# The cross-attention keys computed with stationary tokens and turned by DVE and ACT

## The reference

```python
memn = rms_norm(mem, norm_mem_g[l])
# cross_attend(rms_norm(x, norm2_g[l]), memn, wq, wk, wv, wo):
q = (xn @ wq).reshape(B, S, XA_HEADS, XA_HEAD_DIM)
k = (memn @ wk).reshape(B, M, XA_HEADS, XA_HEAD_DIM)
v = (memn @ wv).reshape(B, M, XA_HEADS, XA_HEAD_DIM)
scores = jnp.einsum('bshd,bmhd->bhsm', q, k).astype(jnp.float32) * (XA_HEAD_DIM ** -0.5)
```

## Time and profile before

| what | value |
|---|---|
| median of 3 runs | 1489.17 us (1489.03 to 1489.21) |
| the profiled execution's own time | 1489.79 us |
| its span, first to last instruction | 1488.0 us |
| PE busy | 1478.4 us (99%) |
| PE's share of the chain of work that ended last | 98% |
| DVE busy | 1025.6 us (69%) |
| ACT busy | 963.5 us (65%) |
| mean granted TensorE clock | 0.999 of full speed |
| DMA, mean over the span | 194 GB/s |

### The profile page before, as it was taken

The page is one execution under the profiler, slowest core; times in us unless marked ns, Lnnn a source line. Parts: engine busy times, 40 slices in busy tenths (PEclk is TensorE's granted clock), DMA queues, the critical chain, the costliest instruction groups (busy, mean ns, idle before and its releaser), DMA issues.

```text
span 1488.0 us, 22342 instructions
## 1 busy us (share of the span) xinstructions
PE 1478.4 (99%) x7186; PEld 1247.9 (84%) x7186; DVE 1025.6 (69%) x1384; ACT 963.5 (65%) x1477; POOL 2.9 (0%) x9
## 2 busy tenths in 40 slices
PE   9999999999999999999999999999999999999997
PEld 8888888888888888888888888888888888888886
DVE  5756666788888566664665776675857676685696
ACT  6644578745555486554767868586766858576974
POOL 0000000000000000000000000000000000000000
PEclk9999999999999999999999999999999999999999
DMA  9756655565556654445555565556555555656554
GB/s 346 259 193 210 218 180 187 199 200 169 175 175 228 197 184 156 156 153 194 190 184 195 186 201 191 190 188 199 187 197 200 186 194 186 199 188 193 195 197 143
DMA packets 81038, 288.93 MB, mean 194 GB/s; under 512 B 9008, under 2 KB 10544, under 8 KB 80096
## 3 DMA queue, kind: packets, MB, share of 16 engines
q1 hardware_dynamic: 76752, 275.68, 55.8%
q10 hardware_dynamic: 3744, 9.30, 1.8%
q0 software_dynamic: 496, 3.34, 0.6%
HBM read 286.19 MB, written 2.10 MB: 194 GB/s over the span
## 4 chain that ended last, share of the span: by engine, by line
PE 98%; ACT 1%; DVE 0%; issue 0%; DMA 0%; ACTq 0%; DVEq 0%
PE ps L282 98%; ACT whi L583 0%; PE ps L343 0%; DMA hl<-in_first_in 0%; DVE wlo L981 0%; PE ps L444 0%; ACT scr L833 0%; DVE sm_ L1349 0%; PE ps L498 0%; DVE tmp L999 0%; ACT scr L956 0%; ACT vm L971 0%; DVE xres L1499 0%; ACTq L118 0%; ACT whi L624 0%
## 5 line engine op out<-in xcount | busy, mean ns | idle before, releaser
L981 DVE TENSOR_TENSOR wlo<-raw,whi 128x1024 fp32r<-128x1024 f32 x516 | 624.7, 1220 | 314.6 <-ACT whi L583 305.6
L583 ACT ACTIVATE whi<-raw 128x1024 fp32r<-128x1024 f32 x516 | 531.4, 1053 | 222.6 <-PE ps L282 216.2
L282 PE MATMUL ps<-whi,xT 128*128 128x512 f32 x1536 | 475.1, 389 | 0.0
L282 PE MATMUL ps<-whi,mixT 128*128 128x512 f32 x1472 | 457.0, 390 | 0.3 <-ACT whi L624 0.3
L282 PEld LDWEIGHTS ps<-whi,xT 128*128 128x128 f32 x1536 | 288.4, 188 | 59.8
L282 PEld LDWEIGHTS ps<-whi,mixT 128*128 128x128 f32 x1472 | 276.8, 188 | 57.9 <-issue 0.6
L282 PE MATMUL ps<-xT,whi 128*128 128x512 f32 x896 | 310.5, 398 | 0.3
L282 PE MATMUL ps<-wlo,xT 128*128 128x512 f32 x768 | 298.8, 389 | 0.0
L282 PE MATMUL ps<-wlo,mixT 128*128 128x512 f32 x736 | 285.1, 389 | 0.0
L282 PE MATMUL ps<-xT,wlo 128*128 128x256 f32 x896 | 234.9, 278 | 0.0
L282 PEld LDWEIGHTS ps<-xT,whi 128*128 128x128 f32 x896 | 162.8, 188 | 32.2 <-DVE wlo L981 0.9
(11 more groups left out here) (186 smaller groups left out, 744.7 us busy)
## 6 DMA issues: line engine op xcount, KB each, us to landing
raw<-in_stream SPq DMA_DIRECT2D x518, 512.0 KB, 3.3
xres<-in_xin ACTq DMA_DIRECT2D x2, 1024.0 KB, 7.3
scr<-in_xt_in ACTq DMA_DIRECT2D x8, 256.0 KB, 3.6
xres<-in_xin POOLq DMA_DIRECT2D x1, 2048.0 KB, 11.9
out_x<-vm SPq DMA_DIRECT2D x8, 256.0 KB, 3.1
raw<-in_stream SPq DMA_DIRECT2D x4, 256.0 KB, 4.3
kT<-in_memt_in ACTq DMA_DIRECT2D x2, 512.0 KB, 5.7
vbuf<-in_memin ACTq DMA_DIRECT2D x1, 1024.0 KB, 10.0
```

The lines of the kernel that those rows point to most:

```text
L282: return nc.tensor.matmul(o, l, r, start=start, stop=stop, skip_group_check=True)
L583: A(whi[:, 2 * pr + s, :], raw[:, 2 * pr + s, :], ACT.Copy).then_inc(hi_done, 1)
L981: V.tensor_tensor(wlo[:, 2 * pr + s, :], raw[:, 2 * pr + s, :], f32(whi[:, 2 * pr + s, :]), ALU.subtract).then_inc(lo_done, 1)
```

## The change

The 16 key chunks become wide. `a["xa_wk"]` is streamed as four groups of 512 output columns with four chunks each. PE writes a group's two banks; ACT scales them by the memory token's factor on the way out (`keep_keys`) into the first half of `vbuf`; DVE turns them in 32x32 blocks into the second half of `vbuf` (`turn_keys`); and ACT moves the blocks into `kT` (`move_keys`, four calls of four instructions to a group). A group's calls stand in the three steps behind it; the calls of the last group stand in the first four steps of stage V. The row of the memory's scales is no longer made. The loops over KM on PE, ACT and DVE are written out, and the places of `hi_tiles` and `load_x` change: the high tiles of `x` now stand behind the second split (`do2`) where they stood between the two, and the load of `x` waits on `xt_lo`, the tiles of the load before.

```diff
@@ PE @@
-            narrow(C_KM // 2, 0, mixT, {}, 2)
-            narrow(C_KM // 2, 1, mixT)
-            with pe.Fori(1, KT // 2) as i:
-                for pr in range(2):
-                    narrow(C_KM // 2 + i, pr, mixT)
+            for n in range(16):
+                wide(C_KM // 2 + n // 2, n % 2, mixT, range(n % 4 * 4, n % 4 * 4 + 4), (4, 2, 4, 0)[n // 4], n % 4 == 0, n % 4 == 3)
@@ ACT @@
-            with act.Fori(0, KT // 2) as i:
-                def load_x():
-
-                    act.wait_ge(lo_done, 4 * i + (2 * C_KM + 4))
-                    act.dma_start(xstage, xt_in[:, ds(2 * i, 2), :]).then_inc(x_in, 16)
-                    copy_hl(0)
-
-                def x_hi():
-                    act.wait_ge(x_in, 16 * i + 16)
-                    hi_tiles(xstage, xT, O_G1, 2 * i, xt_hi)
-
-                step(C_KM // 2 + i, 0, load_x)
-                step(C_KM // 2 + i, 1, lambda: copy_hl(1), x_hi)
+            def load_x(i):
+                if i:
+                    act.wait_ge(xt_lo, 2 * i)
+                act.dma_start(xstage, xt_in[:, 2 * i:2 * i + 2, :]).then_inc(x_in, 16)
+
+            def x_hi(i):
+                act.wait_ge(x_in, 16 * i + 16)
+                hi_tiles(xstage, xT, O_G1, 2 * i, xt_hi)
+
+            def keep_keys(g):
+                for tt in range(TT):
+                    A(km_rows[:, tt, :], ps[:, (4, 2, 4, 0)[g] + tt, :], ACT.Copy, scale=rcol[:, 0, tt:tt + 1]).then_inc(km_kept, 1)
+
+            def move_keys(g, i):
+
+                act.wait_ge(km_turned, 2 * g + 2)
+                for q in range(4):
+                    A(kT[q * 32:(q + 1) * 32, 4 * g:4 * g + 4, :].rearrange("p j (t i b) -> p j t i b", t=TT, i=4)[:, :, :, i, :],
+                      km_blocks[i * 32:(i + 1) * 32, q], ACT.Copy).then_inc(km_moved, 1)
+
+            for n in range(16):
+                def before_split():
+                    if n % 4 == 3:
+                        keep_keys(n // 4)
+                    elif n % 2 == 0:
+                        load_x(n // 2)
+
+                def between():
+                    if n >= 4 and n % 4 < 3:
+                        move_keys(n // 4 - 1, n % 4)
+
+                def behind():
+                    if n % 2:
+                        x_hi(n // 2)
+                    elif n >= 4 and n % 4 == 0:
+                        move_keys(n // 4 - 1, 3)
+
+                step(C_KM // 2 + n // 2, n % 2, before_split, between, behind)
...
             for n in range(8):
+                keys = (lambda: move_keys(3, n)) if n < 4 else None
                 if n % 2:
-                    step(C_V // 2 + n // 2, 1, None, None, lambda: lru_part(n // 2))
+                    step(C_V // 2 + n // 2, 1, None, keys, lambda: lru_part(n // 2))
                 else:
-                    step(C_V // 2 + n // 2, 0, None, lambda: lru_root(n // 2))
+                    step(C_V // 2 + n // 2, 0, None, lambda: lru_root(n // 2), keys)
@@ DVE @@
-                def key(pr):
-                    ch.link(narrow_sum(W_KM + 2 * i + pr, pr, tmp[:, pr, :]))
-                    V.tensor_tensor(kT[:, 2 * i + pr, :], tmp[:, pr, :], row_mem, ALU.mult)
-                def x_lo():
-                    dve.wait_ge(xt_hi, 2 * i + 2)
-                    lo_tiles(xstage, xT, O_G1, 2 * i, xt_lo)
-                step(C_KM // 2 + i, 0, lambda: key(0))
-                step(C_KM // 2 + i, 1, lambda: key(1), x_lo)
+            def x_lo(i):
+                dve.wait_ge(xt_hi, 2 * i + 2)
+                lo_tiles(xstage, xT, O_G1, 2 * i, xt_lo)
+
+            def turn_keys(g):
+                dve.wait_ge(km_kept, 2 * g + 2)
+                if g:
+                    dve.wait_ge(km_moved, 16 * g)
+                for tt in range(TT):
+                    V.transpose(km_blocks.rearrange("p q j t b -> p t j q b")[:, tt], km_rows[:, tt, :]).then_inc(km_turned, 1)
+
+            for n in range(16):
+                step(C_KM // 2 + n // 2, n % 2, None, (lambda: turn_keys(n // 4)) if n % 4 == 3 else None,
+                     (lambda: x_lo(n // 2)) if n % 2 else None)
...
             def v_out(g):
+                dve.wait_ge(km_moved, 64)
```

More of the change, by code:

```diff
@@ L63 @@
 NC = C_F + 2 * NF + NF
-W_KM, W_YU, W_H, W_Q, W_F = 0, 16, 32, 56, 72
+W_YU, W_H, W_Q = 0, 16, 40
 PAN = 1024
@@ L165, in build @@
         first_mem = hl[:].rearrange("p a b -> p (a b)")[:, :KT + T]
-        row_mem = csr[:, 0, :]
+        km_rows = vbuf[:, 0, :].rearrange("p (t c) -> p t c", t=TT)
+        km_blocks = vbuf[:, 1, :].rearrange("p (q j t b) -> p q j t b", q=4, j=4, t=TT)
         zout = vm
@@ L193, in build @@
         x_in, xt_hi, xt_lo = sem("x_in"), sem("xt_hi"), sem("xt_lo")
+        km_kept, km_turned, km_moved = sem("km_kept"), sem("km_turned"), sem("km_moved")
         gw_in, un_ready, uc0_done, uc_ready, yn_ready, gates_done, i_ready = (
@@ L326, in wide, with row_of @@
                         mid()
-            def row_of(n):
-                pe.wait_ge(diag_ready, n + 1)
+            def row_of():
+                pe.wait_ge(diag_ready, 1)
                 for tt in range(TT):
@@ L346, in norm_tr @@
                         last.then_inc(nt_tr, 1)
[L349 to L354, removed]
             def first_use(n, kt, s, k):
@@ L389, in _ @@
                 wide(n // 2, n % 2, mixT, range(4 * kp, 4 * kp + 4), 2 * g, kp == 0, kp == 3,
-                     (lambda: vm_at(n)) if n in (7, 12) else None,
+                     row_of if n == 12 else None,
                      (lambda kt, s, k: first_use(n, kt, s, k)) if n in (2, 4, 6) else None)
-            narrow(C_KM // 2, 0, mixT, {}, 2)
-            narrow(C_KM // 2, 1, mixT)
-            with pe.Fori(1, KT // 2) as i:
-                for pr in range(2):
-                    narrow(C_KM // 2 + i, pr, mixT)
+            for n in range(16):
+                wide(C_KM // 2 + n // 2, n % 2, mixT, range(n % 4 * 4, n % 4 * 4 + 4), (4, 2, 4, 0)[n // 4], n % 4 == 0, n % 4 == 3)
             def wait_for(s, v):
@@ L1012, in inv_root, with diag_of @@
                 ch.link(V.reciprocal(rcol[:, n, :], sm_[:, 1, :]))
-            def diag_of(n, k):
+            def diag_of(n):
                 for tt in range(TT):
@@ L1017, in diag_of, with read_row @@
                 last.then_inc(diag_ready, 1)
[L1019 to L1022, removed]
+            def read_row():
+                dve.wait_ge(row_done, 1)
+                V.tensor_copy(row[:], bankA[:, :T]).then_inc(row_read, 1)
+                dve.wait_ge(row_read, 1)
             def mem_lo(r):
@@ L1057, in rms @@
                 inv_root(n)
-                dve.wait_ge(ident_in_s, 16)
                 if n:
-                    dve.wait_ge(row_read, n)
-                diag_of(n, n)
+                    dve.wait_ge(ident_in_s, 16)
+                    diag_of(n)
             def abs_lambda():
@@ L1127, in vm_out @@
                                     None, ALU.mult)
-            side = {2: lambda: mem_lo(4), 4: lambda: mem_lo(5), (5, 2): lambda: rms(0), 7: lambda: read_row(0, row_mem),
+            side = {2: lambda: mem_lo(4), 4: lambda: mem_lo(5), (5, 2): lambda: rms(0),
                     (2, 2): abs_lambda, (4, 2): log_sigmoid, (7, 2): log_sigmoid_end, (8, 2): angles,
-                    (10, 2): lambda: rms(1), 12: lambda: read_row(1), (12, 2): cosines}
+                    (10, 2): lambda: rms(1), 12: read_row, (12, 2): cosines}
             for n in range(16):
@@ L1575, in weight_stream @@
     ffn += [down[n] for n in range(NG - 3, NG)]
-    parts = [wide_stream(a["xa_wv"][0], order=VM_ORDER), narrow_chunks(a["xa_wk"][0]), yu, wide_stream(v), heads,
+    parts = [wide_stream(a["xa_wv"][0], order=VM_ORDER), wide_chunks(a["xa_wk"][0]).swapaxes(0, 1).reshape(16, P, D), yu, wide_stream(v), heads,
              wide_stream(a["w_out"][0], (2, 3, 0, 1)), narrow_chunks(a["xa_wq"][0]), wide_stream(a["xa_wo"][0])] + ffn
```

4 lines of the change are left out of this document (removed).

## The result

The changed kernel takes 1494.72 us in the median of 7 runs (1492.89 to 1496.25), the kernel before 1489.17 (1489.02 to 1490.13). The ratio is 1.0035, with a 95% interval of 1.0023 to 1.0046: slower by 5.5 us, more than the 0.2% that was named as measurable and above the stated range of 1488.9 to 1493.9. The runs also lie 3.4 us apart, where those of before lie 1.1 apart. The granted clock is the share of TensorE's full speed of 2.4 GHz that the chip lets it run at.

What follows compares the result with a forecast made beforehand. PE was taken as the bound, holding 98% of the span; -1.74 - 0.45 + 0.89 + 0.97 + 3.13 = +2.8 us on the profiled 1489.79 gave 1492.6, forecast as a 1492.0 median, range 1488.9 to 1493.9.

Steps and rivals of the forecast that it cites:

- The two rates: PE's stream in KM: 5.547 us for a narrow chunk, 5.438 for a wide one, a gain of 1.74 us.
- the ring: KM, ACT to DVE to ACT through the `x` load's wait: 22.72 us per four chunks against PE's 21.75, costing 1.86.
- the wait for the last tiles: YU's first chunk, pair 14: low tiles ready at L + 10.80, wanted at L + 7.67, a PE stall of 3.13 us.
- KM's products and the row: PE's stream: wide key chunks save 1.74 us, dropping the four records of the row of scales saves 0.45.
- waits in KM and at YU's start: PE waits on DVE's split: chunk 12 comes 0.89 us late, chunk 16, YU's first, another 0.97.
- The clock falls: Rival, chance 0.07: the stall in YU brings the granted clock down, costing 2.6 us more, 1494.6 us.
- Hand-overs cost more: Rival, chance 0.20: four hand-overs in KM's four chunks cost 0.16 us more each, 0.64 a group, 1494.2 us.
- no wait in V: Stage V's first steps: the last group's moves leave DVE's second split a cover of 1.0 us, cost none.
- No stall at all: Rival, chance 0.05: PE keeps the whole 2.19 us gain without waiting in KM or YU, 1487.0 us.

Runs made afterwards that it cites:

- last version: Changed kernel with the tiles of `x` between the splits in odd steps and YU's first four products paired, two high then two low: 1486.88 us, ratio 0.9986.
- the stalls alone: Kernel before, PE held at pair 14 of YU's first chunk by 1, 3, 5 or 8 DVE dummy instructions: 1490.58, 1493.27, 1494.34, 1495.79 us.
- both repairs: Changed kernel with two buffers for the load of `x` and, in step 15, the last tiles made between the splits, ahead of the turn: 1487.39 us, ratio 0.9988.
- two buffers: Changed kernel, last tiles left in place, with a second buffer for `x` so the load waits for tiles of two loads back: 1489.54 us, ratio 1.0004.
- the tiles between the splits: Changed kernel, one buffer, with high and low tiles of `x` between the splits in odd steps, turn and moves behind the second split: 1487.29 us, ratio 0.9987.
- the last two experiments: Changed kernel with the tiles of `x` between the splits in odd steps, 1487.29 us; then also YU's first four products paired, 1486.88 us.

## Why the prediction was wrong, point by point

The two rates, the ring and the wait for the last tiles are where the prediction put them; one step was priced at nothing, and one term was too small. Forecast +2.8 us, measured +5.5.

| term | forecast | measured | from |
|---|---|---|---|
| KM's products and the row | -2.19 | -2.2 | last version against before |
| waits in KM and at YU's start | +1.86 | +3.0 | 90.00 against 87.0 |
| wait for the last tiles | +3.13 | +3.0 | start to start at 191.00 |
| half clock behind it | 0 | +1.7 | 191.00 to 195.46; 1.6 to 1.8 in the traces of the stalls alone |
| spacing of YU's products behind it | 0 | +0.3 | 0.353 for 0.347 until about 216 |

The measured terms add up to +5.8; the medians say +5.5, the two profiled spans 4.9 with 0.8 of the opening to add.

**The step that failed** is the rival "The clock falls", put at 0.07 with the words that a stall of 3.1 us is shorter than the 5.2 us after which the clock fell at the kernel's end. The end of the kernel gave one case in which the clock fell, and I read it as a lower bound on the idle time that it takes. It was none: one event says nothing of the shortest. The stalls alone show the fall at 2.19 us already, and at 3.10 every run lies at least 1.4 us beyond its stall. In the changed kernel the trace shows it; whether its two fastest runs (1492.89 and 1493.44) paid it too stays open. The price was read too high, 2.6 us for 5.2 us at half clock: the clock is back at 1.00 after 3.4 us, while PE works. With 1.7 us for it the forecast would have been 1493.7, still 1.0 low.

**The term that was mis-sized** is the ring: 22.72 us a group in the forecast, 23.0 and 23.3 in the trace (loads at 121.74, 144.75 and 168.03). Against 16 chunks of 5.438 us, chunk 12 starts 1.65 us late where 0.89 was forecast, and chunk 16 2.99 where it was 1.86. About 0.2 of a group's excess is the load that follows a wait: it goes out 0.09 us after the low tiles' end where 0.04 was taken, and the split starts 0.43 to 0.44 after it where 0.40 was taken, twice a group each. Another 0.13 is a split of 1.09 to the next start in step 4k+2 where 0.96 was taken, though no moves stand directly in front of it. Some 0.3 us once, at step 8, where the split starts 0.72 after the load's issue, has no cause in what I looked at. It belongs to that place in ACT's program and not to the ring: the split of step 8 starts 0.71 to 0.72 after the load's issue in the traces of both repairs, of two buffers and of the tiles between the splits too, where PE's chunks come in time. These small sums decide because chunk 8 was in time by only 0.08 us: three groups late instead of two. So the rival "Hand-overs cost more" was true in kind, with about a quarter of the 0.64 us a group that it took.

**Right:** PE's rates of both kinds of chunk and 88.75 - 87.01 = 1.74 us between them; the row at 0.45 (0.3 by the medians, 0.45 in the trace); the place, cause and length of the wait for the last tiles; no wait in V, where the moves of the last group took nothing visible. The last version keeps a gain of 2.2 us, so the trace's two rates held. With the fixed 2.5 ns a matmul of the Trainium skill, TensorE: Matmul & The Clock Gate, section Back-to-back issue gap, the gain would have been 0.32 + 0.45 us; the runs do not agree with it. What was overlooked in PE's stream is that the removed line also set the spacing of the products behind it; the two rates were read from stretches in which it was right.

**A rival dismissed by a wrong sentence.** "No stall at all" (0.05) says that it needs the last tiles 2 us earlier than any order of these instructions gives. That holds for the order of the change only. With the tiles between the splits, the same instructions on the same one buffer bring them in time, and the kernel takes 1487.29 us.

## What to carry to other kernels

In a pipeline in which one engine's busy time is the span, look for every wait that closes a ring between the two engines that feed it, and add up the ring from start to start, hand-overs included: ACT and DVE were at 67% and 53% in KM and still too late. Work whose consumer is near goes ahead of work whose consumer is far; the same instructions in another order turned 5.5 us of loss into 1.8 of gain. In this kernel a wait of TensorE of 2.2 to 4.5 us cost some 2 us beyond its length, and waits under 1 us left the clock up: put such a term into the sum wherever a forecast has a long wait, and prefer several short waits to a long one.

## What the runs showed of the hardware

- One stall of TensorE of 1.26 us left the granted clock at 1.00, one of 1.98 left it there in the profiled run, one of 2.19 brought it to 0.50 (1.2 GHz). The fall costs a further 1.8 to 2.1 us by the medians, 1.6 to 1.8 in stage YU of the traces, whether the stall is 2.2 or 4.5 us long. The waits of 0.84 and 0.94 us in KM and at YU's start left the clock at 1.00.
- The fall comes late: it shows 0.7 to 1.0 us after PE is back at work in the four traces that have it (in the changed kernel 191.00, and 191.9 by the row 191.00:192.00 at 0.95), so the products right behind a stall still run at full speed and those after them do not.
- The same alternation of 512-column and 256-column products runs at 0.3467 or at 0.3533 us a pair, according to how the first four are ordered behind wide products (the last two experiments). A wait can change it either way: in the changed kernel the pairs behind the wait of 183.04 stand 0.346 apart, those behind that of 191.00 0.353. What sets it stays open.
- A split on ACT takes 0.96 us to the next start, or 1.08 in most places in which block moves on 32 partitions follow it; what picks the one or the other stays open.
